# Splitting each weight chunk with one ScalarE and one VectorE instruction in place of two of each

## What is computed

```python
def swiglu(h, wg, wu, wd):
    return (jax.nn.silu(h @ wg) * (h @ wu)) @ wd
...
    for e in range(N_EXPERTS):
        y = y + gate[:, e:e + 1].astype(xt.dtype) * swiglu(xt, wg[e], wu[e], wd[e])
```

## Time and profile before

| | |
|---|---|
| median of three runs | 1953.15 us (1951.01 to 1954.14) |
| the profiled execution's own time | 1955.25 us |
| its span in the trace | 1953.4 us |
| instructions in the span | 23164 |
| granted TensorE clock, mean | 0.941 |

### The profile page before, as it was taken

One profiled execution on the slowest core, in us unless ns is written; L12 is line 12 of the kernel. 1 busy time (PEld: TensorE's weight loads), 2 busy tenths in 40 slices (PEclk: granted clock), 3 DMA queues, 4 the chain that ended last, 5 costly groups with the idle time before them and its releaser, 6 DMA issues.

```text
span 1953.4 us, 23164 instructions
## 1 busy us (share of the span) xinstructions
PE 1734.1 (89%) x7827; PEld 1402.1 (72%) x7827; DVE 1381.7 (71%) x1844; ACT 1100.3 (56%) x1370; POOL 15.8 (1%) x30
## 2 busy tenths in 40 slices
PE   6878977987999996589899999899899899999995
PEld 4656865866788875478777677687687687776774
DVE  5755756646455555569778788698797797786886
ACT  4343443442444452257667577576676676675773
POOL 1001000000000000000000000000000000000000
PEclk9898987988999997789999999999999999999997
DMA  8424522432546551259889799799799898897992
GB/s 309 147 84 118 169 97 82 151 108 65 163 139 214 175 177 55 86 190 372 305 301 360 279 339 355 265 358 352 259 370 322 281 372 304 302 357 273 346 355 93
DMA packets 232034, 461.42 MB, mean 236 GB/s; under 512 B 7790, under 2 KB 12156, under 8 KB 231852
## 3 DMA queue, kind: packets, MB, share of 16 engines
q1 hardware_dynamic: 229712, 454.32, 66.4%
q0 software_dynamic: 1552, 4.56, 0.9%
q10 hardware_dynamic: 716, 1.85, 0.2%
HBM read 459.65 MB, written 1.05 MB: 236 GB/s over the span
## 4 chain that ended last, share of the span: by engine, by line
PE 77%; DVE 10%; ACT 5%; issue 4%; DVEq 2%; DMA 1%; ACTq 0%; SPq 0%
PE ps L1373 22%; PE ps L1375 22%; PE ps L1374 22%; PE ps L1708 3%; DVE wlo_sb L767 2%; ACT whi_sb L531 2%; PE ps L1685 2%; PE ps L1640 1%; DMA raw_sb<-w_in 1%; PE ps L1398 1%; DVE xT_sb L1328 1%; ACT xhi_sb L739 0%; ACT yg_sb L756 0%; PE ps L1453 0%; PE ps L1667 0%
## 5 line engine op out<-in xcount | busy, mean ns | idle before, releaser
L767 DVE TENSOR_TENSOR wlo_sb<-raw_sb,whi_sb 128x1024 fp32r<-128x1024 f32 (+2 forms) x870 | 1015.5, 1212 | 328.3 <-ACT whi_sb L531 326.2
L531 ACT ACTIVATE whi_sb<-raw_sb 128x1024 fp32r<-128x1024 f32 (+2 forms) x870 | 865.6, 1045 | 562.0 <-PE ps L1375 546.9
L1373 PE MATMUL ps<-whi_sb,xlo_sb 128*128 128x512 f32 (+2 forms) x1568 | 628.5, 401 | 38.2 <-ACT sg_sb L702 10.9
L1374 PE MATMUL ps<-wlo_sb,xhi_sb 128*128 128x512 f32 (+2 forms) x1568 | 613.9, 392 | 0.0
L1375 PE MATMUL ps<-whi_sb,xhi_sb 128*128 128x512 f32 (+2 forms) x1568 | 613.2, 391 | 0.0
L1373 PEld LDWEIGHTS ps<-whi_sb,xlo_sb 128*128 128x128 f32 x1568 | 300.3, 192 | 105.3 <-DVE wlo_sb L767 21.8
L1375 PEld LDWEIGHTS ps<-whi_sb,xhi_sb 128*128 128x128 f32 x1568 | 299.5, 191 | 61.9
L1374 PEld LDWEIGHTS ps<-wlo_sb,xhi_sb 128*128 128x128 f32 x1568 | 300.5, 192 | 59.4 <-issue 2.2
L1373 PE MATMUL ps<-whi_sb,alo_sb 128*128 128x512 f32 x536 | 215.7, 402 | 18.6 <-DVE actv_sb L1202 11.4
L1375 PE MATMUL ps<-whi_sb,ahi_sb 128*128 128x512 f32 x536 | 212.0, 396 | 0.0
L1374 PE MATMUL ps<-wlo_sb,ahi_sb 128*128 128x512 f32 x536 | 211.9, 395 | 0.0
(11 more groups left out here) (258 smaller groups left out, 992.2 us busy)
## 6 DMA issues: line engine op xcount, KB each, us to landing
raw_sb<-moe_wg SPq DMA_DIRECT2D x115, 1024.0 KB, 5.1
raw_sb<-moe_wu SPq DMA_DIRECT2D x112, 1024.0 KB, 5.3
raw_sb<-moe_wd SPq DMA_DIRECT2D x112, 1024.0 KB, 5.1
raw_sb<-w_in SPq DMA_DIRECT2D x40, 1024.0 KB, 5.1
raw_sb<-w_out SPq DMA_DIRECT2D x16, 1024.0 KB, 5.0
raw_sb<-ffn_wg SPq DMA_DIRECT2D x10, 1024.0 KB, 5.1
raw_sb<-ffn_wu SPq DMA_DIRECT2D x10, 1024.0 KB, 5.0
raw_sb<-ffn_wd SPq DMA_DIRECT2D x10, 1024.0 KB, 5.1
```

Source lines behind the costliest of these rows:

```text
L531: nc.scalar.activation(whi[i % SPLIT][:, c:c + k // 2, 0:n], raw[i % RAW][:, c:c + k // 2, 0:n], ACT.Copy).then_inc(hi_ready, 1)
L767: op = V.tensor_tensor(wlo[i % SPLIT][:, c:c + k // 2, 0:n], raw[i % RAW][:, c:c + k // 2, 0:n], whi[i % SPLIT][:, c:c + k // 2, 0:n], ALU ...
L1373: mm(out, lo, whi[i % SPLIT][:, c, 0:chunk.n], start=first, stop=False)
L1374: mm(out, hi, wlo[i % SPLIT][:, c, 0:chunk.n], start=False, stop=False)
```

## The change

Each chunk has one ScalarE instruction that rounds all four blocks, and one VectorE instruction that subtracts all four, where it had two of each over two blocks. `hi_ready` is raised once per chunk. The VectorE instruction waits for the whole of `whi`.

```diff
@@ act_hi
-            for c in range(0, k, k // 2):
-
-                nc.scalar.activation(whi[i % SPLIT][:, c:c + k // 2, 0:n], raw[i % RAW][:, c:c + k // 2, 0:n],
-                                     ACT.Copy).then_inc(hi_ready, 1)
+            nc.scalar.activation(whi[i % SPLIT][:, 0:k, 0:n], raw[i % RAW][:, 0:k, 0:n], ACT.Copy).then_inc(hi_ready, 1)
@@ dve_lo
-            for c in range(0, k, k // 2):
-
-                dve.wait_ge(hi_ready, 2 * c0 + 2 * i + (2 if c else 1) + 2 * per * l)
-                op = V.tensor_tensor(wlo[i % SPLIT][:, c:c + k // 2, 0:n], raw[i % RAW][:, c:c + k // 2, 0:n],
-                                     whi[i % SPLIT][:, c:c + k // 2, 0:n], ALU.subtract)
-            op.then_inc(lo_ready, 1)
+            dve.wait_ge(hi_ready, number(c0, i + 1, per, l))
+            V.tensor_tensor(wlo[i % SPLIT][:, 0:k, 0:n], raw[i % RAW][:, 0:k, 0:n], whi[i % SPLIT][:, 0:k, 0:n],
+                            ALU.subtract).then_inc(lo_ready, 1)
```

## The result

The changed kernel takes **1985.82 us** (median of 4 runs, 1984.75 to 1986.85) against 1953.39 us for the kernel before (4 runs, 1951.01 to 1954.14): a ratio of 1.0168, 95% interval 1.0150 to 1.0186. It is 32 us slower. The forecast was 1977 us, 24 us slower, in a range of 1964 to 1996 us.

What follows compares the result with a forecast made beforehand. The prediction took TensorE (busy 89%) as the bound: 16.6 us in the experts, 3 in the hybrid, mixer and dense parts and 4 for the clock make 23.6 us on 1953.15, so 1977 us, range 1964 (+11) to 1996 (+43).

Steps and rivals of the forecast that it cites:

- Durations: Every chunk: merged whi 1.91 us, wlo 2.29 us; whi start to wlo end 4.25 us, before 3.46.
- The last `actv`: In each expert, TensorE's 1.43 us wait for the last actv grows by 0.79 us to 2.2 us.
- The gather: In each expert, two splits on one chain add 1.48 us; TensorE's 0.90 us wait for wlo becomes 2.4 us.
- `sg` and `yg`: In each expert, TensorE's two waits for ScalarE, before sg and yg, each become 0.10 us shorter.
- Steady chunks: Ordinary chunks of an expert: no cost, as the buffers give the split 5.4 us against 4.25 us.
- the thin cover: Mid-expert actv: some 0.4 us left before TensorE wants it; once gone, each tenth of a us costs 4.8 us.
- rival 3: Mid-expert actv is later than its cover by 0.3 us: 14 us more, 1991 us; chance 0.08.
- Hybrid, mixer and dense parts: Outside the experts: +3 us, between 1 and 5; two places in each hybrid layer cost 0.79 us each, 3.2 us.
- Transfers: SyncE's transfers start up to 0.79 us later, but the ring of six buffers covers it: no cost.
- The clock: TensorE in experts: 11 us lost at four in ten of 16 longer waits, 7 us (a third) back at scatters; net +4.
- rival 2: TensorE's clock falls at nearly every longer wait, nothing returned: 27 us from falls, 2000 us; chance 0.08.
- The rule on fixed costs: VectorE: by the skill's formula a merged subtraction saves 0.16 us a chunk, 68 us if VectorE were the bound.

Runs made afterwards that it cites:

- e11: Kernel before, with actv ahead of wlo, the gather's work two steps earlier, yg ahead of the last whi, sg ahead of its whi: 1875.70 us.
- e13: Changed kernel, merged everywhere, with the same four orders as e11: 1883.86 us.
- e1: Changed kernel with only ScalarE's instruction merged, VectorE keeping two, both after the whole of whi: 1986.68 us.
- e2: Changed kernel with only VectorE's instruction merged, ScalarE keeping two and raising hi_ready after the second: 1984.46 us.
- e4: Changed kernel with three of each expert's 42 chunks (31st, 41st, 42nd) back to two instructions of each: 1950.34 us.
- e7: Changed kernel with actv ahead of the wlo of its step in an expert and the gather's VectorE and ScalarE work two steps earlier: 1919.26 us.
- e8: Kernel before with the same two changes of order as e7: 1914.91 us.
- e5: Changed kernel with 8 unused matmuls ahead of each expert's two long waits, for the last actv and the last wlo: 1961.18 us.
- e3: Changed kernel merged in the experts alone, with two instructions of each in the chunks outside them: 1979.72 us.

## Why the prediction was right, point by point

- **Durations.** 1.91 us was estimated for the merged `whi`, 1.92 stands in the list; 2.29 us for `wlo`, 2.29 measured. The latency was put at 4.25 us and is 4.25.
- **The last `actv`.** 2.2 us expected, 2.22 measured. **The gather.** 2.4 us expected, 2.29 measured. `sg` and `yg` are 0.1 us shorter, as said. The sum was 16.6 us; the table of waits gives 16.0.
- **Steady chunks.** No new wait, so the thin cover of 0.4 us held (rival 3 is out). With the four orders, in e11, a cover of this kind broke.
- **Hybrid, mixer and dense parts.** +3 us; the trace shows 2.8 ahead of the first expert, but in this trace the number came out in part by luck. Three of the four places named grew about as forecast (2.89 to 3.67 us twice, 6.82 to 7.43). The fourth shrank from 6.46 to 4.19 us,

```profile
314.36 0.69 PE L1447 MATMUL ps<-P_sb,xT_sb 128*128 128x64 f32 x2 [4.19 <-ACT xT_sb L554]
```

behind a stretch at the lower level that the trace before does not have (mean clock 0.57 from 296 to 304 us, where it was 1.00 from 294 to 302). TensorE's waits ahead of the first expert sum to 150 us in both traces, and its loss at the lower level grows from 52.3 to 55.5 us. That the term itself is right, e11 and e13 show: with equal clocks the same four places give 3.0 us, for 3.2 forecast.
- **Transfers.** Still 5.1 to 5.3 us to landing, and no wait of ScalarE for an expert's transfer. Right.
- **The clock.** This is the term that was mis-sized: "Net +4 us", measured +12.3. The step took four in ten of the longer waits to bring a fall, 11 us; ten of 16 did, 16.7 us. It took a third of the 23 us at the scatters to come back, 7 us; 4.4 came back, and not by scatters that escaped the fall, as the step had it, but by four falls half as long. Both misses went the same way and come to 8.3 us, about what separates 24 from 32 us; the profiled execution, which is 29.5 us slower, has 1.1 us less in the experts than its waits and clock add up to. Each fall's price, 1.7 us, was right, and so was the scatter's, 2.9 us: 6.8 us at the lower level, of which about 1 us was idle time, half of the rest lost. The "four in ten" and the "third" were choices and not derived, so that the sum came this near is luck in part. Of rival 2, a fall at nearly every longer wait with nothing returned (27 us, chance 0.08), nearly half came true. The range's upper end of +43 does not follow from the terms it names: 16.6 + 3, half of rival 2 (13.5) and rival 3's 14 give 47 us. The measured 32 us lie below both.
- **The rule on fixed costs.** The Trainium skill's rule (VectorE: DVE Perf Modes, "The TRN2 errata") that one large tile pays a fixed cost once is borne out in size only in part: a merged subtraction saves 0.07 us where the estimate from the page's formula was 0.16 (28 us of VectorE's busy time in all, for 68). The time went the other way.

e1 and e2 show that the start of VectorE is the cause. e4, e7 and e8 show at which chunks it counts, and e5 that the rest in the experts is the clock. e3 is the weaker witness for how the loss is divided: its trace is 2.1 us shorter than the changed kernel's ahead of the experts, but also 3.4 us shorter in the experts, where the code is the same and 31.7 us are lost at the lower level for 35.3. What decides at which waits the clock falls stays open.

## What to carry to other kernels

Two instructions of half the size on two engines in a row are a pipeline. Merging them saves what a pair costs beyond one large instruction, here 0.07 and 0.10 us, and adds nearly half of the first engine's work to the latency, here 0.79 us: count the saving only where that engine is the bound, and the latency at each place where the engine that is the bound waits behind the result. Look at what stands behind a slow instruction in each queue before tuning the instruction: moving four short pieces of work ahead of splits that nobody waited for yet was worth 78 us, where the form of the split was worth 32. Both figures have the clock in them, 23 us of the 78 and 12 of the 32. And add to every wait of TensorE what a fall of its clock costs, as a share of the cases in the trace.

## What the runs showed of the hardware that was not expected

- A wait of the same length may bring a fall of TensorE's clock or not: 2.21 us in the second expert did (mean 0.79 over 8 us), 2.22 us in the fourth and fifth did not (1.00). The kernel before met it at the same point of all eight experts, each of which took 136.5 to 136.6 us. With other lengths, 137.5 to 141.9 us, it came and went. That the length decides is a reading of these traces that no run tested by itself.
- The unchanged kernel's own time moves with its clock. Of its 29 runs beside the experiments 22 were at 1952 to 1959 us with a mean clock of 0.938 to 0.942. The other seven took 1936.18 to 1950.13 us: 1936.18 with 0.951, 1942.72 with 0.947, four at 1946 to 1948 with 0.946 or 0.948, and 1950.13 with 0.942.
- Matmuls without a use made a kernel faster: 128 of them took 21 to 25 us off the changed kernel, 88 of them some 21 us off the kernel before.
